# The causal mask of a forgetting attention: an add on VectorE in place of a product on TensorE

## What is computed

```python
s = jnp.einsum('bhqd,bhkd->bhqk', q_b, k).astype(F32) * scale
s = s + c_b[..., :, None] - cum[..., None, :]
q_pos = start + jnp.arange(Q_BLOCK)
s = jnp.where(k_pos[None, :] <= q_pos[:, None], s, NEG_INF)
p = jax.nn.softmax(s, axis=-1)
return jnp.einsum('bhqk,bhkd->bhqd', p.astype(v.dtype), v)
```

## Time and profile before

| | |
|---|---|
| runs | 3587.87, 3588.87, 3589.56 us; median 3588.87 |
| profiled execution, own time | 3582.91 us |
| its span | 3581.1 us |
| TensorE busy | 2990.6 us (84%) |
| VectorE busy | 835.7 us (23%) |
| ScalarE busy | 639.9 us (18%) |
| stages "fa0" and "fa1" | 148.7 to 203.2 us, 343.0 to 397.2 us |

### The profile page before, as it was taken

How to read it: one execution, slowest core, us unless ns; L and a number is a source line. 1 busy time by engine, 2 the same in 40 slices (tenths; PEclk the granted TensorE clock), 3 DMA queues, 4 the chain that set the end, 5 groups by cost and what they waited for, 6 DMA issues and landing times. The chain is left out here.

```text
span 3581.1 us, 33057 instructions
## 1 busy us (share of the span) xinstructions
PE 2990.6 (84%) x12650; PEld 1489.5 (42%) x12650; DVE 835.7 (23%) x2158; ACT 639.9 (18%) x1369; POOL 191.2 (5%) x146
## 2 busy tenths in 40 slices
PE   7999858888859999995888888398879887989987
PEld 3544532222214444443222222256456454455554
DVE  1221321111111211212111110317323342053054
ACT  2211300000011000001000000216224241042043
POOL 0000010000000000001000000100100102011011
PEclk9999969898989999996989899699989988999999
DMA  5411059999984233232999999310000101120110
GB/s 200 190 48 71 26 198 394 391 394 394 394 319 158 94 118 118 94 118 79 388 391 393 395 393 394 118 41 14 13 24 25 36 24 47 47 65 24 47 42 30
DMA packets 191589, 604.45 MB, mean 169 GB/s; under 512 B 9941, under 2 KB 24218, under 8 KB 191338
## 3 DMA queue, kind: packets, MB, share of 16 engines
q1 hardware_dynamic: 165360, 537.15, 39.5%
q10 hardware_dynamic: 20858, 46.88, 4.3%
q0 software_dynamic: 5248, 18.75, 1.4%
HBM read 559.16 MB, written 43.52 MB: 168 GB/s over the span
## 5 line engine op out<-in xcount | busy, mean ns | idle before, releaser
L1038 PE MATMUL psum<-ring,arena 128*64 128x512 f32 x2048 | 564.1, 703 | 176.6 <-DMA ring<-in_expert_w_gu 174.7
L463 PE MATMUL psum<-ring,XT 128*128 128x512 f32 (+3 forms) x1216 | 478.5, 554 | 12.3 <-ACT arena L1598 6.6
L453 PE MATMUL psum<-XT,ring 128*128 128x512 f32 (+1 forms) x1152 | 444.2, 547 | 4.2 <-POOLq L1845 2.4
L1038 PEld LDWEIGHTS psum<-ring,arena 128*64 128x64 f32 x2048 | 159.0, 159 | 538.1 <-issue 300.4
L463 PEld LDWEIGHTS psum<-ring,XT 128*128 128x128 f32 x1216 | 229.6, 190 | 252.8 <-issue 219.6
L553 PE MATMUL psum<-ring,arena 128*128 128x512 f32 x704 | 311.2, 603 | 10.0 <-ACT arena L588 5.7
L453 PEld LDWEIGHTS psum<-XT,ring 128*128 128x128 f32 x1152 | 219.2, 191 | 228.1 <-issue 218.8
L652 PE MATMUL psum<-arena 128*128 128x512 f32 (+8 forms) x704 | 256.3, 481 | 42.0 <-ACT arena L706 33.7
L1051 PE MATMUL psum<-ring,arena 128*64 128x512 f32 x1024 | 233.8, 598 | 25.9 <-DMA ring<-in_expert_w_down 25.9
L1112 DVE TENSOR_TENSOR arena<-arena,psum 64x512 f32<-64x512 f32 x64 | 44.2, 690 | 751.6 <-ACT arena L1115 751.6
L553 PEld LDWEIGHTS psum<-ring,arena 128*128 128x128 f32 x704 | 135.2, 194 | 181.3 <-issue 167.0
(11 more groups left out here) (216 smaller groups left out, 2173.2 us busy)
## 6 DMA issues: line engine op xcount, KB each, us to landing
ring<-in_expert_w_gu SPq DMA_DIRECT2D x128, 2048.0 KB, 12.2
ring<-in_expert_w_down SPq DMA_DIRECT2D x64, 2048.0 KB, 13.1
ring<-in_ada_w SPq DMA_DIRECT2D x12, 2048.0 KB, 8.1
ring<-in_fox_w_in SPq DMA_DIRECT2D x8, 2048.0 KB, 8.7
arena<-xg_dram ACTq DMA_DIRECT2D x64, 256.0 KB, 6.6
y_dram<-arena ACTq DMA_DIRECT2D x128, 128.0 KB, 5.9
ring<-in_ret_w_in SPq DMA_DIRECT2D x8, 2048.0 KB, 10.4
ring<-in_c_in_w SPq DMA_DIRECT2D x8, 2048.0 KB, 7.8
```

The lines of the kernel that those rows point to most:

```text
L453: i = pe.matmul(ps[0][0:cols_[1] - cols_[0], 0:ntok], w[:, c, cols_[0]:cols_[1]], x[:, c, tok:tok + ntok], start=(c == 0), stop=(c == k - 1))
L463: i = pe.matmul(ps[0][:, 0:width], x[:, c, t * P:(t + 1) * P], w[:, c, c0:c0 + width], start=(c == 0), stop=(c == k - 1))
L1038: i = pe.matmul(psum[side * BR:(side + 1) * BR, 0:FF], self.XGT[:, 4 * part + c, :], w[:, c, side * FF:(side + 1) * FF], start=(part == 0 ...
```

## The change

One argument of the two forgetting stages:

```diff
                        lambda h, i: [(0, (i + 1) * P, QT[0:66, h, i * P:(i + 1) * P], KT[0:66, h, 0:(i + 1) * P])],
                        lambda i: range(i + 1),
                        lambda h, kt: V[:, kt, h * DH:(h + 1) * DH], lambda q: GT[:, q, :], lambda q: GT[:, q, :],
-                       add=lambda i: [(i * P, (i + 1) * P, causal)], masks_on_pe=True)
+                       add=lambda i: [(i * P, (i + 1) * P, causal)], masks_on_pe=False)
```

## The result

The changed kernel is slower: 3609.11 us, the median of 6 runs (3599.82 to 3613.46), against 3588.48 for the kernel before (6 runs, 3587.87 to 3595.67). The ratio is 1.0051, with a 95% interval from 1.0036 to 1.0067. The forecast was 3590, its range ended at 3600, and slower by over 0.2% had been given a chance of 0.16.

A forecast was written before the change was run, and what follows sets the result against it. TensorE, nearly full, bounds the kernel now; VectorE's queue would in the wide half. Per stage 0.12 − 3 × 0.02 + 0.51 = 0.57 us, 1.1 for two, gives 3584.0, or 3590.0 on the median's level; range 3583 to 3600.

The forecast's parts named there:

- The price of the mask on each engine: Per unit in the forgetting stages: TensorE loses 0.22 us of mask product, VectorE gains 0.34 us for an add lasting 0.30.
- The period: Steady part of a forgetting stage, two heads or eight units: 12.69 us laid out against 12.71 now.
- The bound changed hands in the wide half: In units with 384 and 512 keys, the limit passes from TensorE (needing only 5.25 us) to VectorE's queue.
- The ends of a stage: Start and end of each forgetting stage: first exponential 0.12 us later, last stretch 12.78 in place of 12.27, 0.51 more.
- The sum at full clock: Per forgetting stage 0.12 − 3 × 0.02 + 0.51 = 0.57 us more, for the two stages 1.1 us.
- the third rival: TensorE's granted clock falls in the forgetting stages because it idles more: 4.1 us, total 3594.4; chance 0.06.
- a clock under 1.00: Sign of a wrong prediction: TensorE's granted clock in the two forgetting stages below 1.00.
- The new waits are single ones of about a microsecond: Argument against a fall of TensorE's clock in the forgetting stages: its added idle times are isolated, about a microsecond each.
- the first exponential comes 0.12 later: At a forgetting stage's start: scores ready 0.22 us sooner, maximum 0.34 longer, so ScalarE's first exponential is 0.12 us later.
- the price, 4.1 us: Cost of a clock fall: ten microseconds at 0.83 per forgetting stage, 2 × 10 × (1/0.83 − 1) = 4.1 us.
- The second rival: Units with 384 and 512 keys pay all four VectorE adds, nothing returns: 10.9 us, total 3599.8; chance 0.15.
- TensorE as the bound: TensorE keeps setting the pace in the forgetting stages, so time falls by 14.1 us to 3574.8; chance 0.08.

The follow-up runs named there:

- the run with four masks back: Changed kernel with masks of the first four units of each forgetting stage as TensorE products again, other 28 as VectorE adds: 3618.79 us, ratio 1.0085.
- the reverse: Against the kernel before, only the first four units of each forgetting stage masked by VectorE adds, other 28 by products: 3605.38 us, ratio 1.0049.
- the filled: Changed kernel plus an identity-by-mask product into a bank nothing reads, behind each unit's scores in the forgetting stages: 3594.80 us, ratio 1.0026.
- waiting kernel: Kernel before, all masks as products, plus four unread exponentials of 640 columns at the start of ScalarE's part of each stage: 3598.88 us, ratio 1.0028.

## Why the prediction was wrong

**The price of the mask on each engine** was right: 0.22 us per unit on TensorE, an add of 0.293 us.

**The period** was right: 12.69 laid out, 12.55 to 12.63 measured, a little below the 12.71 of before. The bound changed hands in the wide half as described. The waits of the changed kernel in one period, against the earlier trace rows:

```profile
PEld psum L670 <- DVE arena L748: 2.9, 3, 1.2
...
ACT arena L706 <- DVE sm L720: 2.2, 4, 0.9
DVE psum L717 <- PE psum L652: 2.0, 2, 1.2
```

VectorE waits for TensorE for 2.0 us where it was 3.9 (for the mask product); TensorE's weight loads wait 2.9 us for VectorE's scaling where it was 0.8, and ScalarE waits for the maxima. TensorE is busy for 10.91 us of 12.63 and VectorE for 10.03 (about 10.5 had been forecast).

**The ends of a stage** were right in size where the clock held: 0.20 more at the start (0.12 forecast), and from the last 384-wide scores to the end 203.30 − 190.67 = 12.63 in the run with four masks back (12.78 forecast, 12.27 before).

**The sum at full clock**, 0.57 us per stage, was somewhat high: with adds 53.67, with products 53.57 where both have the early load and fillers (not the same ones at the start), and 53.17 with products and no fillers. So the stage costs between 0.1 and 0.5 us more with adds, 0.2 to 1.0 for both, in place of 1.1. All adds at full clock without any filler were never measured.

**What failed** is the step that left TensorE's clock at 1.00: the third rival, which had a chance of 0.06, is what happened, and the prediction had named a clock under 1.00 as a sign that it was wrong. Two sentences of that rival were wrong. "The new waits are single ones of about a microsecond": in the steady part they are, but at a stage's start the step "the first exponential comes 0.12 later" counted only how late VectorE's work is, and not that TensorE reaches the wait 0.88 us earlier (four masks of 0.22). 1.09 + 0.88 + 0.12 = 2.09 could have been summed from the trace of before, and 2.10 was measured. And the price, 4.1 us, took one piece of mixed clock (0.83 for ten microseconds) as a model; added to the forecast of 3590.0 it gives 3594.1, not the 3594.4 written. In fact the clock was 0.50 for 20 us at the start and 10 at the end of each stage, and at half clock TensorE, which has slack at full clock, sets the pace alone (busy for 4.00 us of 4.00 in the windows shown from 153 to 173 us). The periods and projections at half clock add up to 6.7 + 6.6 + 2.2 + 2.1 + 2.1 + 1.7 = 21.4 us, of which some 0.7 belongs to the ends anyhow: all of the loss in the profiled run.

**The second rival**, whose time of 3599.8 is the nearest to the measured one, was wrong in its mechanism: at full clock no stage with adds was longer by more than a microsecond than the same stage before (55.41 against 54.49 at most, in the kernel with 64 fillers), where this rival had 5.4. **TensorE as the bound** was wrong as argued. The rule of the Trainium skill behind the second rival ("VectorE: DVE Perf Modes", rules for kernel authors: keep the count of chained operations low) agrees with these runs on VectorE itself, where each add takes its 0.293 us, and not on the stage, where 32 of them cost about 0.5 us of 53.7 at most as long as the clock held.

The Trainium skill ("TensorE: Matmul & The Clock Gate", part 1) says that the array clock is gated by a monitor of how busy TensorE has been, with half rate for an idle one. The falls at the starts of stages fit that, as in the kernel made to wait. The long falls do not: the clock stayed at 0.50 for 74 us of one stage while TensorE was busy for 71.09 of 74.21 us. That the kernel before was near a fall could not be told from its own rows of 1.00; it shows in the run that waited 1.4 us longer.

**What stays open.** Why the clock fell in one stage and not in the other of the same run, with equal queues and waits (the run with four masks back), isn't settled; neither is why it came back after 10 to 20 us in most falls, in one stage after 68 us, and in two not before their end. In all falls of kernels that had at least 28 mask or filler products behind the start (the reverse, the filled and the waiting kernel) it came back within 17 us; that is an observation on five stages, and three kernels without them (changed, no mask, early table load) had falls of 17 to 20 us that ended too. The fall at the stage's end was not tried by itself: the fillers there went in together with others.

## What to carry to other kernels

Work taken from TensorE is a gain only while the granted clock stays where it is, and a profile at 1.00 doesn't say how close the edge is. When an edit makes TensorE's queue shorter, sum up the new length of its longest wait at each stage's start and end (the old wait, plus what TensorE no longer does ahead of it, plus what the others do in addition), and price the case that the clock halves with the engine's own load at half rate over the stretch that follows. Where such a wait can't be avoided, a few products that nothing reads in it, with the table load moved ahead, cost some tenths of a microsecond and removed the loss: 3587.68 against 3588.89 before, no difference clear of noise. The change itself is then worth nothing; the fastest kernel, by 0.17%, kept the masks as products.

## What was not expected of the hardware

- Once down, the granted clock can stay at 0.50 for 74 us and more while TensorE is busy for 96% of the time (71.09 of 74.21 us, second stage of the run with four masks back).
- A kernel with 14 us less of TensorE's work in two stages, and nothing in its place, has a median 14 us above the one with it.
- The spread of a kernel's runs is itself a sign of the clock: 49.9 us for the one with four masks back and 44.1 for the one without masks (granted clock 0.919 and 0.916 in their fastest runs, 0.904 in their slowest), 9.5 for the kernel before with the early table load and fillers (0.921 to 0.924).
